# The token mixer of a two-layer hybrid decoder, rebuilt around running products of forget gates

## What is computed

```python
def mixer(h, s_hg, s_lru, s_conv, lb, ...):
    q_pre, f_pre, i_pre, g_pre, xr, gr = jnp.split(h @ w_in, splits, axis=-1)   # 6 x 512 columns
    q = silu(q_pre); v = i_pre                       # 4 heads of 128
    log_f = logaddexp(log(lb), log1p(-lb) + log_sigmoid(f_pre))  # f = lb + (1-lb)*sigmoid
    k = (1.0 - lb) * sigmoid(-f_pre)
    # group 1: gated linear recurrence S_t = f_t * S_(t-1) + k_t v_t^T,  o_t = q_t S_t
    o, s_hg_new = hgrn2_chunked(q, k, v, log_f, s_hg)
    o = o * rsqrt(mean(o * o) + EPS) * hg_norm_g * silu(g_pre)
    # group 2: width-4 causal convolution, two gates r and ig, linear recurrence over the tokens
    xc, conv_new = causal_conv(xr, s_conv, conv_w, conv_b)
    a = exp(-8 * softplus(-lru_lambda) * r); u = sqrt(1 - a * a) * (ig * xc)
    hs = scan(a, u);  lru_out = hs * gelu(gr)
    return concat([o, lru_out]) @ w_out
```

## Time and profile before

| | us |
|---|---|
| three timed runs | 1711.54, 1715.77, 1716.29 |
| median | 1715.77 |
| span of the profiled execution, first to last instruction | 1714.0 |

### The profile page before, as it was taken

How to read it: one execution, slowest core, us unless ns; L and a number is a source line. 1 busy time by engine, 2 the same in 40 slices (tenths; PEclk the granted TensorE clock), 3 DMA queues, 4 the chain that set the end, 5 groups by cost and what they waited for, 6 DMA issues and landing times.

```text
span 1714.0 us, 24614 instructions
## 1 busy us (share of the span) xinstructions
PE 1604.6 (94%) x8844; PEld 1376.9 (80%) x8844; DVE 1358.8 (79%) x1264; ACT 1011.9 (59%) x840; POOL 160.5 (9%) x130
## 2 busy tenths in 40 slices
PE   6895889999996798999999999999999999999997
PEld 5895789998896687887888888888888788788885
DVE  5997665666697748888888888888888888888985
ACT  4644343334545326767766776776676777677672
POOL 2245400000144510000000000000000000000000
PEclk8996899999997679999999999999999999999999
DMA  8451245545343017998998998998998998998990
GB/s 260 130 160 61 92 151 182 171 164 179 124 142 105 25 57 266 368 355 291 375 359 275 370 370 281 373 355 293 362 364 288 357 368 295 360 361 299 352 341 26
DMA packets 212918, 433.00 MB, mean 253 GB/s; under 512 B 7064, under 2 KB 62800, under 8 KB 212880
## 3 DMA queue, kind: packets, MB, share of 16 engines
q1 hardware_dynamic: 208176, 421.59, 69.9%
q0 software_dynamic: 1792, 5.42, 1.0%
q10 hardware_dynamic: 2912, 5.47, 0.9%
HBM read 426.57 MB, written 5.95 MB: 252 GB/s over the span
## 4 chain that ended last, share of the span: by engine, by line
PE 76%; DVE 14%; ACT 5%; issue 3%; DMA 1%; PEld 0%; POOL 0%; DVEq 0%; ACTq 0%; SPq 0%; PEldq 0%
PE ps L1338 22%; PE ps L1340 22%; PE ps L1339 22%; DVE w_lo L773 3%; PE ps L1607 3%; ACT w_hi L482 2%; PE ps L1654 1%; PE ps L1354 1%; DVE xc L927 1%; DVE lev L899 1%; DVE sc L915 1%; DMA out_dram<-hstate 1%; DVE lev L901 1%; DVE xc L1034 1%; DVE y_f L1245 1%
## 5 line engine op out<-in xcount | busy, mean ns | idle before, releaser
L773 DVE TENSOR_TENSOR w_lo<-raw,w_hi 128x2048 fp32r<-128x2048 f32 x401 | 921.7, 2311 | 188.7 <-ACT w_hi L482 181.7
L482 ACT ACTIVATE w_hi<-raw 128x2048 fp32r<-128x2048 f32 x401 | 763.5, 1917 | 332.9 <-PE ps L1340 208.7
L1338 PE MATMUL ps<-w_hi,xg 128*128 128x512 f32 x896 | 359.4, 401 | 7.4 <-DVE w_lo L773 7.4
L1340 PE MATMUL ps<-w_hi,xg 128*128 128x512 f32 x896 | 354.5, 396 | 0.0
L1339 PE MATMUL ps<-w_lo,xg 128*128 128x512 f32 x896 | 354.1, 395 | 0.0
L1338 PE MATMUL ps<-h_hi,w_hi 128*128 128x264 f32 x736 | 216.5, 294 | 23.5 <-DVE h_lo L800 15.5
L1339 PE MATMUL ps<-h_lo,w_hi 128*128 128x264 f32 x736 | 211.5, 287 | 0.0
L1340 PE MATMUL ps<-h_hi,w_lo 128*128 128x264 f32 x736 | 211.5, 287 | 0.0
L1338 PEld LDWEIGHTS ps<-w_hi,xg 128*128 128x128 f32 x896 | 169.0, 189 | 52.5 <-DVE w_lo L773 16.7
L1340 PEld LDWEIGHTS ps<-w_hi,xg 128*128 128x128 f32 x896 | 168.8, 188 | 40.1
L1339 PEld LDWEIGHTS ps<-w_lo,xg 128*128 128x128 f32 x896 | 169.2, 189 | 36.1
(11 more groups left out here) (282 smaller groups left out, 1831.1 us busy)
## 6 DMA issues: line engine op xcount, KB each, us to landing
raw<-in_moe_w_dram SPq DMA_DIRECT2D x336, 1024.0 KB, 6.2
raw<-in_ffn_w_dram SPq DMA_DIRECT2D x33, 1024.0 KB, 5.5
raw<-in_w_in_dram SPq DMA_DIRECT2D x24, 1024.0 KB, 5.5
raw<-in_w_out_dram SPq DMA_DIRECT2D x8, 1024.0 KB, 4.9
out_dram<-hstate POOLq DMA_DIRECT2D x2, 2048.0 KB, 10.5
x_rows<-in_x_prompt_dram SPq DMA_DIRECT2D x1, 1024.0 KB
out_dram<-y_rows ACTq DMA_DIRECT2D x2, 512.0 KB
out_dram<-s_fin POOLq DMA_DIRECT2D x2, 256.0 KB, 9.8
```

The costliest lines, as they stand in the source:

```text
L482: act.activation(w_hi[:, s, :], raw[:, r, :], ACT.Copy).then_inc(hi_made, 1)
L773: dve.tensor_tensor(w_lo[:, s, :], raw[:, r, :], w_hi[:, s, :].bitcast(F32), ALU.subtract).then_inc(split, 1)
L1338: pe.matmul(out, l_hi, r_hi, start=start, stop=False)
L1340: return pe.matmul(out, l_lo, r_hi, start=False, stop=stop)
```

## The change

- Levels: no logs, no exponentials, no `lev` buffers. `key` and `qd` (query times its own forget gate) are multiplied in place, level after level, by running products of forget gates (`extend`), three DVE instructions a level. Level k's operands can be made only after PE has read those of level k-1. POOL has no arithmetic left in the mixer.
- ACT applies `Sigmoid` and `Silu` straight from PSUM in `z_out`, gelu is one instruction (`Gelu_apprx_tanh`). The columns come in the order f, q, xr, g, v, gr; z has three banks instead of four; the eight gate products are made in pairs behind units 7 to 10, the value transposes behind unit 10; levels run behind units 4 to 11.
- Sample states have a buffer of their own and are loaded by POOL's queue, for layer 0 at the start of the kernel and for layer 1 after layer 0's store. Their decay moves from POOL to ACT (32 instructions); values are spread by four products with a broadcast weight, without diagonals.
- The waits of PE on its own products behind the weight units go; ACT's wait is on `z_done`, `y_done` or `used` directly (`freed`).
- The output projection of the first four column blocks starts with the four LRU chunks, ahead of the wait for the head norm.

ACT takes z out of PSUM:

```diff
             def z_out(l, n):
                 act.wait_ge(z_done, 24 * l + n + 1)
-                bank, h = ps[:, n % 4, :], n % 4
+                bank, h = ps[:, n % Z_BANKS, :], n % 4
...
+                if group == 0:
...
+                    act.activation(forget[:, h, :], bank[:, 0:T], ACT.Sigmoid)
+                    act.activation(key[:, h, :], bank[:, 0:T], ACT.Sigmoid, scale=-1.0
+                                   ).then_inc(z_free, 1)
```

DVE, the levels and its order in the input projection:

```diff
+                def extend(k):
+                    half = 1 << k
                     parts = lambda a: a[:, :, 0:NPROMPT].rearrange(
                         "p h (n two m) -> p h n two m", two=2, m=half)
+                    kv, qv, fv = parts(key), parts(qd), parts(forget)
+                    even, odd = fv[:, :, :, 0, half - 1:half], fv[:, :, :, 1, half - 1:half]
+                    wide = [P, HEADS, NPROMPT // (2 * half), half]
+                    dve.wait_ge(sc_done, SCORES * l + 2 * k + 4)
+                    dve.tensor_tensor(kv[:, :, :, 0, :], kv[:, :, :, 0, :], odd.broadcast_to(wide),
+                                      ALU.mult).then_inc(lev_ready, 1)
+                    dve.tensor_tensor(qv[:, :, :, 1, :], qv[:, :, :, 1, :], even.broadcast_to(wide),
+                                      ALU.mult).then_inc(lev_ready, 1)
+                    dve.wait_ge(lev_ready, 14 * l + 2 * k + 1)
+                    link(dve.tensor_tensor(odd, odd, even, ALU.mult))
...
+                for u in range(IN_UNITS + SPLIT - 1):
...
+                    if u >= LEVEL_LAG:
+                        extend(u - LEVEL_LAG)
+                        take_level(u - LEVEL_LAG)
+                    if EARLY[l] <= u < IN_UNITS + 2:
                         lo(ib + u)
...
+                    if CONV_LAG <= u < CONV_LAG + HEADS:
+                        conv(u - CONV_LAG)
```

PE, the input projection:

```diff
                 for u in range(IN_UNITS):
                     pe.wait_ge(split, ib + u + 1)
...
-                    pe.wait_ge(z_done, 24 * l + t + 1)
-                    pe.sem_inc(used, 1)
...
+                    if u >= 4:
+                        level(u - 4)
...
+                    if u >= GATE_LAG and u < GATE_LAG + HEADS:
+                        gate_pair(u - GATE_LAG)
```

PE, the tail, `spread_value`, the output projection and, last, the down projection of the dense block:

```diff
+                turn(19, key, 1, kd_turned)
+                pe.wait_ge(z_free, Z_BANKS + 24 * (l + 1))
                 pe.wait_ge(gates_ready, 8 * (l + 1))
+                in_chunk(0)
+                pe.wait_ge(kd_ready, l + 1)
+                turn(20, key, 0, kd_turned)
+                in_chunk(1)
                 pe.wait_ge(st_landed, 16 * (l + 1))
                 for b in range(NSAMPLE):
                     for h in range(HEADS):
                         col = NPROMPT + b
                         ins = pe.matmul(ps[:, h, col:col + 1], hstate[:, HEADS * b + h, :],
-                                        zq[:, h, col:col + 1], start=True, stop=True)
+                                        qd[:, h, col:col + 1], start=True, stop=True)
...
+                    for h in range(HEADS):
+                        ins = pe.matmul(ps[:, 5 + b % 3, P * h:P * h + P],
+                                        v_s[:, h, b:b + 1].broadcast_to([P, P]), ident[:, :],
+                                        start=True, stop=True)
...
+                for c in range(4):
+                    pe.wait_ge(split, ob + c // 2 + 1)
+                    out_part(c, MERGE_ORDER[:HEADS], True, False)
                 pe.wait_ge(o_root, l + 1)
...
+                for c in range(DC):
+                    if c < 4:
+                        out_part(c, MERGE_ORDER[HEADS:], False, True).then_inc(y_done, 1)
+                    else:
...
+                        out_part(c, MERGE_ORDER, True, True).then_inc(y_done, 1)
+                    spread_value(c)
...
                     ins.then_inc(y_done, 1)
-                pe.wait_ge(y_done, s * DC + 2 * DC)
-                pe.sem_inc(used, 1)
```

More of the change, by code:

```diff
@@ L605, in mixer @@
-                for n in range(3, 8):
-                    gate(n)
+                    if u == GATE_LAG + HEADS + 2:
+                        v_out(0)
+                        v_out(1)
+                    if GATE_LAG + SPLIT <= u < GATE_LAG + SPLIT + HEADS:
+                        gate_pair(u - GATE_LAG - SPLIT)
                 act.wait_ge(gates_ready, 8 * (l + 1))
                 for j in range(HEADS):
-                    act.activation(zx[:, j, :], lev[1][:, j, :], ACT.Tanh,
+                    act.activation(zx[:, j, :], zf[:, j, :], ACT.Tanh,
@@ L625, in merge_high @@
+                have_table(ACT.Ln)
                 def merge_high(n):
@@ L1116, in ff_add, with ff_step @@
                                       ).then_inc(x_sum, 1)
-            def ff_step(i, k, add, first=False):
+            def ff_step(i, k, add):
                 b = FF_BASE + 2 + 3 * k
@@ L1356, in norm, with project @@
                 ins.then_inc(ssq_done, 1)
[L1358 removed]
+            def project(base, j, bank, parts=None):
                 _, s, _, _ = unit_of(base)
@@ L1380, in scores @@
+                def scores(n, right, c, across=False, half=0):
+                    bank = product(n)
                     for h in range(HEADS):
                         rc = 1 if across else c
-                        ins = pe.matmul(ps[:, 4 + n % 4, P * h:P * h + P],
-                                        left[:, h, P * c:P * c + P],
-                                        right[:, h, P * rc:P * rc + P], start=True, stop=True)
+                        s, t = P * c, P * rc
+                        ins = pe.matmul(ps[0:P - half, bank, P * h + half:P * h + P],
+                                        key[:, h, s:s + P - half], right[:, h, t + half:t + P],
+                                        start=True, stop=True)
@@ new lines, in gate_pair @@
+                def gate_pair(j):
+                    pe.wait_ge(conv_ready, HEADS * l + j + 1)
+                    if j == 0 and l == 0:
+                        pe.wait_ge(gw_landed, 16 * 8)
+                    for kind in range(2):
+                        if j:
+                            pe.wait_ge(gates_ready, 8 * l + 2 * j + kind - 1)
+                        pe.matmul(ps[:, GATE_BANK[kind], 0:T], gate_w[:, l, kind, j, :],
+                                  xc[:, j, :], start=True, stop=True).then_inc(gates_done, 1)
@@ L1395, in mixer, with turn @@
+                def turn(n, src, c, done):
+                    bank = product(n)
+                    for h in range(HEADS):
+                        ins = pe.transpose(ps[:, bank, P * h:P * h + P],
+                                           src[:, h, P * c:P * c + P], ident[:, :])
+                    ins.then_inc(done, 1)
                 for u in range(IN_UNITS):
@@ L1441, in mixer @@
-                pe.wait_ge(v_ready, l + 1)
-                pe.wait_ge(kd_tok_ready, l + 1)
-                pe.wait_ge(sc_taken, PRODUCTS * (l + 1))
-                for h in range(HEADS):
-                    for c in range(2):
-                        ins = pe.matmul(ps[:, 4, P * h:P * h + P], k_tok[:, c, h, :],
-                                        v_tok[:, c, h, :], start=(c == 0), stop=(c == 1))
-                ins.then_inc(fin_done, 1)
-                pe.wait_ge(gates_ready, 8 * (l + 1))
@@ L1451, in mixer @@
-                for h in range(HEADS):
-                    pe.matmul(ps[:, h, 0:P], v_tok[:, 0, h, :], sc[:, 0, h, :], start=True,
-                              stop=True)
-                    pe.matmul(ps[:, h, P:2 * P], v_tok[:, 0, h, :], sc[:, 2, h, :], start=True,
-                              stop=False)
-                    pe.matmul(ps[:, h, P:2 * P], v_tok[:, 1, h, :], sc[:, 1, h, :], start=False,
-                              stop=True)
-                pe.wait_ge(qf_ready, l + 1)
@@ L1470, in mixer @@
                 pe.sem_inc(o_done, 1)
+                pe.wait_ge(kd_tok_ready, 2 * (l + 1))
+                for h in range(HEADS):
+                    for c in range(2):
+                        ins = pe.matmul(ps[:, 7, P * h:P * h + P], k_tok[:, c, h, :],
+                                        v_tok[:, c, h, :], start=(c == 0), stop=(c == 1))
+                ins.then_inc(fin_done, 1)
                 def spread_value(b):
-                    pe.wait_ge(diag_ready, 2 * (NSAMPLE * l + b + 1))
                     if b < 3:
```

676 lines of the change are left out of this document (296 added, 380 removed).

## The result

The changed kernel takes 1637.53 us (median of four runs, 1635.75 to 1638.58) against 1713.65 for the kernel before (four runs on the same chip): ratio 0.9553, 95% interval 0.9538 to 0.9567. The forecast was 1647, with a range of 1632 to 1670. The profiled execution spans 1636.8 us, 77.2 less than before. In the table the tail ends, and the out stage begins, with the first product behind PE's wait for the head norm. In the output projection, first halves are the products of the four LRU chunks in the first four column blocks, second halves those of the heads.

A forecast was written before the change was run, and what follows sets the result against it. The tails were taken as bound by a serial chain at a low clock. Layers -34.4 and -32.5, dense block -6.5, stores +1, hand-overs +3: -69 from 1714.0 is 1645, with the median 1.8 above the span 1647; range 1632 to 1670.

The forecast's parts named there:

- Input projection, the stops (-6.6): Input projection: twelve PE stops of 0.55 us go, -6.6 in each layer.
- the third (1.3): Layer 0's input projection: a new wait for query times gate, made behind the setup arithmetic, +1.3 with the first take.
- DVE keeps up (7.9 against 8.5): Input projection, units 7 to 10: DVE needs 7.9 us a unit against PE's 8.5, so PE sets the pace.
- Rival A: Input projections: DVE is the bound, some 6 us more a layer, total 1659 to 1673; chance 0.13.
- The tail (25.4 + 3.1): From level 7's end: products through Exp 25.4 us, states kept at 11.75; gate multiplications and low halves with hand-overs 3.1.
- Rival (D): Tail: the clock stays up, so a larger gain, total below 1634; chance 0.05.
- Even at the old sizes they end before it: Tail: DVE's gate arithmetic, sqrt and scans, even at old sizes, end before the state products, which set the end.
- Ln to merge as the chain: Tail, behind the head sums: Ln 1.14, load 1.28, Exp 1.08, then gates and low halves 3.1, all in the chain.
- Out stage (23.5): Out stage: rest of first block 0.5, three halves 4.3, four blocks 11.6, eight spreads 7.1, together 23.5 us.
- Dense block (-6.5): Dense block: eleven stops are 8.1 us, the loop's jump may stay (0.39 x 5); between -6 and -8, taken as -6.5.
- Stores (+1): Layer 1's store starts some 6 us later against the norm; routing's buffer clearing waits for it: 0 to +3, taken +1.
- Hand-overs (+3): Both chains: some ten more hand-overs of 0.1 to 0.3 us than written out, +3.

The follow-up runs named there:

- e1b: Changed kernel with TensorE's waits on its own last product, plus a semaphore count, put back in input projections, output projections and dense block: 1657.88 us.
- e2: Changed kernel with POOL given two 128x512 subtractions at each of levels 0 to 5 in both layers' input projections: 1651.54 us.
- w1: Changed kernel with the 32 state products 112 columns wide instead of one, samples in falling order, all results in bank 4: 1628.07 us.
- e8: Changed kernel with eight 128x512 subtractions on POOL in each tail, from the end of level 7: 1638.51 us.
- e7: Changed kernel with the head norm's Ln, table load and Exp replaced by one inverse-root activation: 1635.00 us.
- e6: Changed kernel without early first halves: the output projection's first four column blocks made in one piece behind the head norm's wait: 1650.01 us.
- v2: Changed kernel with 112-column state products, shorter DVE chain, one inverse root, a later high half, and POOL's small stores ahead of the sample states' store: 1627.48 us.
- e3: Changed kernel with 28 of the 32 one-column state products taken away: 1629.79 us.
- e5: Changed kernel with the prompt's final state ahead of the state products and ACT's second key copy ahead of the square root: 1641.74 us.
- v1: Changed kernel with half the state products behind the last input-projection unit, DVE and ACT reordered, one inverse root, a later high half: 1637.60 us.

## Why the prediction was right, and where it was off

The mechanisms held; the total came 9.5 us lower than forecast, inside the range. Step by step:

- **Bound.** A serial chain at a low clock: right, as the new chain came out term by term (below). No run puts single parts of the old tail back, so how its 33 and 36 us split among them (logs, POOL's work, gates, transposes) is not shown. Level 7 ended 97.3 and 93.5 us after the first product of its layer (96.0 and 93.0 forecast).
- **Input projection, the stops (-6.6).** Mis-sized: 0.55 was a whole unit's difference; between products it is 0.46, and e1b gives back 5.4 in layer 1 and 3.5 in layer 0. The waits (2.06 and 1.33 for 1.8 and 1.4) were right, but the third (1.3) did not come, and behind the first the clock fell, which the sum did not have (some 1.5). In layer 0 these two nearly cancel, so that -0.5 for -1.8 looks like the stops' term alone; that is in part luck.
- **DVE keeps up (7.9 against 8.5).** Right: DVE waits for PE, 6.3 over seven levels, and no level waits for DVE. Rival A's price was low: 8 to 9 a layer (e2), not 6, as I had doubled the extensions alone and left out the clock.
- **The tail (25.4 + 3.1).** From the end of level 7 in layer 0: products 3.57 (3.6 forecast), states 11.4 (11.75), final state 3.55 (3.6), sums 2.6 (2.9), Ln, load and Exp 3.55 (3.5), merge 2.95 (3.1), together 27.7 for 28.5. Layer 1 is the better one, -36.3 for -34.2, for its states took 9.45: the term "I keep their time as it is" is a price of the clock's; it came out 0.4 to 3.0 lower, by the execution. Rival (D), the clock staying up in the tail, did not come by itself; w1 brings it about.
- **"Even at the old sizes they end before it."** Wrong (e8): the scans would have ended 0.9 and 2.8 late.
- **Ln to merge as the chain.** Only half right: 6.2 us of first halves on PE run beside it and end at the same time, so neither alone sets the end (e7: 0 for 2.4; e6: +6.1).
- **Out stage (23.5).** Right: 24.7 from the start of the second halves, 23.9 from the last low half.
- **Dense block (-6.5).** -8.4. The 8.1 for eleven stops was high: the ten boundaries between products before the change add up to 7.1. And I left the loop's jump (0.39 x 5) in place. e1b shows it returning only together with the stop (1.06 and 0.66 in turn): without a stop, queued products hide it. 1.0 of the 8.4 is not given back by e1b; the stage itself varied by as much in runs that don't touch it (195.1 to 196.0), so that is left open.
- **Stores (+1).** The store of the states took 9.2 to land (10.5), and the wait came; what ended it was the last of the small stores that POOL issues behind it:

```profile
543.90 1.76 DVE L1099 MEMSET h_tok<- 128x2048 f32 x1 [3.94 <-DMA out_dram<-outs_t]
```

The logits' copies stand 15.8 us behind the norm's first product for 14.4 before, 1.4 lost; with the store order of v2 they stand at 14.6. But the routing as a whole got shorter by 1.0, as its small products ran at a higher clock (those of the expert positions 2.2 us from the first to what follows them, 3.9 before), and it took 37.6 to 40.2 in other runs with the same order of stores. The term was right and too small to see.
- **Hand-overs (+3).** Not there: PE is idle for 0.15 us in a tail, so hand-overs lie under its work. This (3.0), the dense block (1.9) and layer 1's tail (2.1) are most of the 9.5.
- **Untouched parts.** The experts took 1.5 longer. 0.8 of it is in the first, where the granted clock was lower (0.71 over its first 10 us, 0.78 before); the rest (130.2 each for 130.1) no run explains; the start lay between 25.3 and 28.1 in all runs, whatever the kernel.

## What to carry to other kernels

Where an engine stops to count, price the stop and its count by the gap between products, and ask what queued work hides once the stop is gone (here the loop's jump). When work is moved off one engine, look at what its silence is worth to the neighbour: twelve subtractions on POOL cost DVE and PE 8 to 9 us a layer. And a stage where TensorE is full but its granted clock is low is not finished: look for narrow products, and widen them before moving them (here 6.1 us for widening, nothing that can be told for moving half of them).

## What the runs showed of the hardware

- 32 products of 128x128 by one column took 8.8 to 11.4 us, by the place where TensorE's clock fell to 1.2 GHz in them; by 112 columns they took 7.30 each time and the granted clock stayed at 1.00 through the tail. While the clock was up, a product took 0.23 at either width.
- What follows such a stretch pays too: the final state's eight products of 128 columns took 3.4 to 3.8 for 2.02, the four head sums up to 3.3 for 1.95, and 3.5 to 3.9 where PE had also been idle ahead of them (e3, e5, v1).
- Behind the wait for the third bank of z in layer 0 (1.7 to 2.1) the granted clock fell for 3.41 us in nine runs; in e2, v1, v2 (1.9, 1.9, 1.7) and e1b (1.2) it did not. The same wait of PE is not always followed by the fall.
- DVE's scans took nearly twice as long beside POOL's subtractions (5.58 for 2.87 for four), a two-operand instruction of 528 columns 1.66 for 0.71. A product of 1056 columns beside the same work took 1.26, as without it, and there POOL's subtraction took 2.39 instead of 1.61 (e8).
- A wait of TensorE on its own last product cost 0.22 between products, and the count behind it another 0.24.
